# Second layer of a two-layer trunk: VectorE turns three of ten probability blocks of a head, and the low part of y moves to GpSimd

## The reference, cut to what matters

```python
for i in range(DEPTH):                       # 2 layers, 8 heads of 128, 512 tokens, width 1024
    hdn = rms_norm(x, norm_g[i])
    # layer 0: block attention with rotary; layer 1: forgetting attention
    q, k, v, z = split(hdn @ w_in)           # 1024 x 4096, per head 4 x 128 columns
    # layer 1, per head:
    sc = (q @ k.T) * scale + (c[..., :, None] - c[..., None, :])   # c: cumulative log-forget
    p = softmax(where(kpos <= tq, sc, -inf)) # 512 x 512, lower triangle
    y = p @ v
    x = x + (merge_heads(y) * silu(z)) @ w_out[i]
```

## Time and profile before

| | |
|---|---|
| median of 3 runs | 547.85 us (547.6 to 548.28) |
| the profiled execution | 548.04 us, span in the trace 546.0 us |
| PE busy | 538.5 us, 99% of the span |
| DVE busy | 411.2 us, 75% |
| ACT busy | 293.3 us, 54% |
| POOL busy | 301.6 us, 55% |

### The profile page before, as it was taken

The page is one execution under the profiler, slowest core; times in us unless marked ns, Lnnn a source line. Parts: engine busy times, 40 slices in busy tenths (PEclk is TensorE's granted clock), DMA queues, the critical chain, the costliest instruction groups (busy, mean ns, idle before and its releaser), DMA issues.

```text
span 546.0 us, 9781 instructions
## 1 busy us (share of the span) xinstructions
PE 538.5 (99%) x2963; PEld 498.4 (91%) x2963; DVE 411.2 (75%) x1042; ACT 293.3 (54%) x863; POOL 301.6 (55%) x357
## 2 busy tenths in 40 slices
PE   6999999999999999999999999999999999999998
PEld 5999999999999999888898999999999999998887
DVE  4678999999999999973563777878787878788331
ACT  6748282928282828272545473737374747464400
POOL 3874564646464646453645486747474747476300
PEclk9999999999999999999999999999999999999999
DMA  9914323231313131223513345525241534232021
GB/s 262 250 27 127 101 59 97 59 97 58 96 58 96 58 96 59 95 86 118 128 27 80 97 102 74 120 61 130 52 121 54 116 57 121 73 105 84 26 96 59
DMA packets 78540, 50.22 MB, mean 92 GB/s; under 512 B 4256, under 2 KB 71592, under 8 KB 78512
## 3 DMA queue, kind: packets, MB, share of 16 engines
q1 hardware_dynamic: 78496, 49.87, 33.8%
q10 hardware_dynamic: 16, 0.00, 0.0%
HBM read 47.75 MB, written 2.12 MB: 91 GB/s over the span
## 4 chain that ended last, share of the span: by engine, by line
PE 97%; DMA 1%; ACT 0%; DVE 0%; SPq 0%; issue 0%
PE banks L379 27%; PE banks L381 27%; PE banks L380 27%; PE banks L509 6%; PE banks L495 3%; PE banks L484 2%; PE banks L483 2%; PE banks L482 2%; DMA first_raw<-in_a_w_in_dram 1%; PE banks L416 1%; PE banks L536 0%; PE banks L535 0%; ACT hT_hi L670 0%; PE banks L467 0%; SPq L333 0%; DVE w_lo L885 0%
## 5 line engine op out<-in xcount | busy, mean ns | idle before, releaser
L1160 POOL TENSOR_TENSOR w_lo<-w_raw,w_hi 128x512 fp32r<-128x512 f32 x146 | 188.4, 1305 | 84.0 <-ACT w_hi L638 84.0
L379 PE MATMUL banks<-w_hi,hT_hi 128*128 128x384 f32 x512 | 173.5, 339 | 0.5 <-DVE w_lo L885 0.3
L381 PE MATMUL banks<-w_hi,hT_lo 128*128 128x384 f32 x512 | 171.8, 336 | 0.0
L380 PE MATMUL banks<-w_lo,hT_hi 128*128 128x384 f32 x512 | 171.8, 335 | 0.0
L947 DVE STREAM_TRANSPOSE banks<-qkn 32x256 f32<-32x256 f32 x240 | 109.4, 456 | 3.6
L379 PEld LDWEIGHTS banks<-w_hi,hT_hi 128*128 128x128 f32 x512 | 96.7, 189 | 2.3 <-DVE w_lo L885 0.7
L380 PEld LDWEIGHTS banks<-w_lo,hT_hi 128*128 128x128 f32 x512 | 96.7, 189 | 0.6
L381 PEld LDWEIGHTS banks<-w_hi,hT_lo 128*128 128x128 f32 x512 | 96.5, 189 | 0.0
L684 ACT ACTIVATE junk<-banks 128x128 bf16<-128x128 f32 x128 | 34.0, 272 | 112.0 <-PE banks L381 111.8
L638 ACT ACTIVATE w_hi<-w_raw 128x512 fp32r<-128x512 f32 x148 | 89.0, 638 | 8.9 <-PE banks L381 5.4
L1013 DVE RECIPROCAL gz<-gz 128x128 f32<-128x128 f32 x64 | 54.3, 908 | 0.7 <-ACT gz L736 0.7
(11 more groups left out here) (119 smaller groups left out, 915.9 us busy)
## 6 DMA issues: line engine op xcount, KB each, us to landing
w_raw<-in_b_w_in_dram SPq DMA_DIRECT2D x64, 256.0 KB, 3.6
w_raw<-in_a_w_in_dram SPq DMA_DIRECT2D x52, 256.0 KB, 2.9
w_raw<-in_w_out_dram SPq DMA_DIRECT2D x32, 256.0 KB, 2.7
first_raw<-in_a_w_in_dram SPq DMA_DIRECT2D x12, 256.0 KB, 5.7
cos_t<-c_rows SPq DMA_DIRECT2D x8, 256.0 KB, 3.6
out_dram<-xs SPq DMA_DIRECT2D x7, 256.0 KB, 2.0
xs<-in_x_dram SPq DMA_DIRECT2D x3, 512.0 KB, 5.9
xs<-in_x_dram SPq DMA_DIRECT2D x2, 256.0 KB, 3.1
```

Source lines behind the costliest of these rows:

```text
L379: pe.matmul(dst, ah, bh, start=first and m == 0, stop=False)
L380: pe.matmul(dst, ah, bl, start=False, stop=False)
L381: mm = pe.matmul(dst, al, bh, start=False, stop=last and m == n - 1)
L1160: pool.tensor_tensor(w_lo[:, slot, k, :], raw, f32(w_hi[:, slot, k, :]), ALU.subtract).then_inc(wlo_set, by)
```

## The change

Three edits, all in layer 1 and all for heads 0 to 6 (head 7 is left as it was, `by_dve` is false there).

1. PE's `turn_probs` leaves out the blocks of row tile 3 at key tiles 1, 2 and 3. DVE turns them in a new `turn_last_probs`, by 32x32 squares into the SBUF tile r_row: 16 transposes of 32x32 and 16 of 32x64. It stands behind `norm_qk` of tile 2 and ahead of `split_v` of tile 3, and signals last_turned.
2. ACT's and DVE's `split_probs` treat these blocks apart: in the second and third group the part from PE is read from PSUM, the part from DVE from r_row, so each engine has two instructions more. ACT waits for last_turned in the second group.
3. `low_y` in layer 1 moves from DVE, ahead of `silu_part`, to POOL, behind `rstd_qk` of tile 1.

```diff
+FIRST_BY_DVE = 1
+        def late_part(js):
+            return r_row[:, 0:P] if js[0] == 1 else r_row[:, P:3 * P]
+        def by_dve(layer, h):
+            return layer == 1 and not (isinstance(h, int) and h == HEADS - 1)
 # PE, turn_probs
                         for t in range(j, TILES):
+                            if by_dve(layer, h) and t == TILES - 1 and j >= FIRST_BY_DVE:
+                                continue
                             mm = pe.transpose(...)
 # ACT, split_probs
                     act.wait_ge(p_turned, 3 * g + n + 1)
-                    act.activation(pT_hi[:, c:c + w], banks[:, PT_AT[js[0]][0], 0:w], ACT.Copy).then_inc(pThi_set, 1)
+                    late = P * sum(j >= FIRST_BY_DVE for j in js) if by_dve(layer, h) else 0
+                    hi = act.activation(pT_hi[:, c:c + w - late], banks[:, PT_AT[js[0]][0], 0:w - late], ACT.Copy)
+                    if late:
+                        act.wait_ge(last_turned, h + 1)
+                        hi = act.activation(pT_hi[:, c + w - late:c + w], late_part(js), ACT.Copy)
+                    hi.then_inc(pThi_set, 1)
 # DVE, split_probs: likewise, a second subtraction that reads late_part(js)
 # DVE, new
+            def turn_last_probs(layer, h):
+                g = HEADS * layer + h
+                dve.wait_ge(probs_set, TILES * g + 1)
+                row = P_COL[TILES - 1]
+                for js in ((1,), (2, 3)):
+                    ...
+                    for a in range(QUADS):
+                        for b in range(QUADS):
+                            turned = dve.transpose(keys[b * QUAD:(b + 1) * QUAD, :, a * QUAD:(a + 1) * QUAD],
+                                                   tokens[a * QUAD:(a + 1) * QUAD, :, b * QUAD:(b + 1) * QUAD])
+                turned.then_inc(last_turned, 1)
 # DVE, period
-                if layer == 1:
-                    late_y(layer, h)
                 for n in range(4):
                     silu_part(layer, h, n)
                 split_v(layer, h + 1, 1 - s, 2)
                 norm_qk(layer, h + 1, 2)
+                if by_dve(layer, h):
+                    turn_last_probs(layer, h)
                 split_v(layer, h + 1, 1 - s, 3)
                 split_probs(layer, h)
 # POOL, period
-                if layer == 0 and not (isinstance(h, int) and h == 0):
+                if not (isinstance(h, int) and h == 0):
                     low_y(layer, h - 1)
```

More of the change, by code:

```diff
@@ L167, in build_trunk @@
         p_turned = sem("p_turned")
+        last_turned = sem("last_turned")
         pThi_set = sem("pThi_set")
@@ L987, in split_probs @@
                     dve.wait_ge(pThi_set, 3 * g + n + 1)
-                    dve.tensor_tensor(pT_lo[:, c:c + w], banks[:, PT_AT[js[0]][0], 0:w], f32(pT_hi[:, c:c + w]),
-                                      ALU.subtract).then_inc(pTlo_set, 1)
+                    late = P * sum(j >= FIRST_BY_DVE for j in js) if by_dve(layer, h) else 0
+                    lo = dve.tensor_tensor(pT_lo[:, c:c + w - late], banks[:, PT_AT[js[0]][0], 0:w - late],
+                                           f32(pT_hi[:, c:c + w - late]), ALU.subtract)
+                    if late:
+                        part = slice(c + w - late, c + w)
+                        lo = dve.tensor_tensor(pT_lo[:, part], late_part(js), f32(pT_hi[:, part]), ALU.subtract)
+                    lo.then_inc(pTlo_set, 1)
+            def turn_last_probs(layer, h):
[3 more added lines that the diff above has]
+                for js in ((1,), (2, 3)):
+                    if js[0] < FIRST_BY_DVE:
+                        continue
+                    n = len(js)
+                    tokens = probs[:, row + js[0] * P:row + (js[-1] + 1) * P].rearrange("p (j c) -> p j c", j=n)
+                    keys = late_part(js).rearrange("p (j c) -> p j c", j=n)
+                    for a in range(QUADS):
[3 more added lines that the diff above has]
+                turned.then_inc(last_turned, 1)
             def gate_y(layer, h):
```

## The result

The changed kernel takes 588.89 us (median of 5 runs, 587.69 to 590.47) against 547.99 us before: a ratio of 1.0746, 95% interval 1.0726 to 1.0766. It is slower by 41 us, and 14 us slower than the forecast of 575.

A forecast was written before the change was run, and what follows sets the result against it. TensorE, busy 99% of the span and 97% of the chain, was taken as the bound. First period 5.05, six periods of 3.65 and tail 0.5 make 27.4 us on 547.85: 575.3, range of all cases 561 to 580.

The forecast's parts named there:

- Part 1: PE's transposes: three fewer for each of seven heads save 2.3 us, the whole possible gain, 0.42%.
- Part 2, X: Time of DVE's 32 small transposes in a period, 222 and 256 ns each before small corrections, without overlap: 7.7 us.
- (a): Low weights behind ACT's wait are complete at E + 4.1, and PE's next qkv cannot start earlier.
- (b): Probabilities: two more DVE instructions add about 0.15; values can start at E + 2.0 and end at E + 3.95.
- E: End of DVE's last small transpose in a period: 25.6 if nothing else shifts, 26.6 with the loop closed.
- (c): Way round through DVE: norm of tile 0 makes the maxima start 1.0 later; period 30.7, 3.65 over 27.06.
- (d): Layer 1's first period, with no such delay behind it: period of 32.1, 5.05 over.
- (e): Passage into last: PE reaches the scores at about 7.5, DVE is ready at 8.0, costing 0.5.
- Part 3: Moving low_y from DVE to POOL: cost zero, by 0.1, covered by POOL's idle ahead of a weight chunk.
- Rivals 1 and 2: Small transposes overlap (3.65 us a period): 546.9, chance 0.06; each costs what a large one does (15.0): 626, chance 0.05.
- the estimate X = 4.0: Skill page's 1.0417 ns a column plus about 75 ns per instruction for DVE's transposes: 548 to 549 us.
- Rival 3: DVE's small transposes partly cheaper, between 4.7 and 6.9 us a period: 554 to 569 us, chance 0.12.

The follow-up runs named there:

- w67_first: Changed kernel with ACT's weight chunks 6 and 7 moved ahead of its split of the probabilities: 581.21 us, ratio 1.0596.
- warm_pe: Changed kernel with 16 matmuls of 512 columns that nobody reads filling PE's wait ahead of values: 579.79 us, ratio 1.0578.
- turn_only: Changed kernel without edit 3, so DVE turns three blocks and low_y stays on DVE: 588.31 us, ratio 1.0725.
- low_only: Kernel before with edit 3 alone: low_y on POOL in layer 1, PE turns all ten blocks: 548.85 us, ratio 1.0012.
- warm_w67: Changed kernel with 12 filler matmuls on PE ahead of values and ACT's weight chunks 6 and 7 ahead of its split: 573.78 us, ratio 1.0474.
- early_turn: Changed kernel with DVE's 32 transposes moved ahead of the gate's reciprocals, behind invert_sums: 601.85 us, ratio 1.0969.
- two_blocks: Changed kernel with DVE turning two of the ten blocks and PE eight: 552.31 us, ratio 1.008.
- unused_turns: Changed kernel where PE turns all ten blocks and DVE's 32 transposes are done but nobody reads them: 578.17 us, ratio 1.0533.
- two_w67: Changed kernel with DVE turning two blocks and ACT's weight chunks 6 and 7 ahead of its split of the probabilities: 558.64 us, ratio 1.0188.
- three_late_first: Changed kernel, three blocks on DVE, with DVE's subtractions from SBUF ahead of those from PSUM: 585.97 us, ratio 1.0697.

## Why the prediction was wrong

By its own steps:

- **Part 1**, PE's transposes: 139 of them are left, 2.3 us less work. Right, and without effect while PE waits.
- **Part 2, X**: 7.7 us forecast; the row at 423.20 has 7.44 for the 32. 202 and 236 ns against 211 and 245, 9 ns each, with 13 ns between them and no overlap. Right. The rule of the Trainium skill on held instructions, by which one whose input or output starts in another quadrant waits until the earlier ones have finished ("VectorE: DVE Perf Modes", section on two Vector instructions with no wait between them), agrees with these rows too.
- **(a) and (b), what follows E.** The mechanism held: ACT idled 5.12 in `split_probs`, the low weights are not what PE met last. A term was mis-sized: "two more instructions, about 0.15". From the first instruction behind E to `values` are 2.97 (430.68 to 433.65), not 2.0. The subtraction of 256 columns with both operands in SBUF took 1.38 beside POOL and 0.41 without it. These 0.97 are on every period; w67_first took back 7.7 us. The Trainium skill has the rule ("SBUF — State Buffer", section on the two separate sides): a DVE instruction with two SBUF inputs and a GpSimd instruction that reads SBUF hold a shared port exclusively, and the later one blocks for the whole of the other. The rows agree: 1.38 when it starts inside a POOL instruction, 0.41 when it starts behind one. The prediction had priced the two instructions by their columns.
- **The step that failed: (b), in two of its terms, and with it (c).** The first is the 0.15 just named, which measured 1.1. The second is that `values`, once started, "end at E + 3.95". Every sum took PE's work after a wait at the pace of before. After the waits of 3.4 us PE ran at PEclk 0.50, `values` took 3.7 to 3.9 in place of 1.92, and in every second head the first six matmuls of `qkv` were slow as well. In (c) the norm of tile 0 was to hold the maxima. It ended at 412.61, 12.0 after the start of `values`, as the forecast's loop has it (10.1 - 2.0 + 1.61 + 2.49 = 12.2), but PE's scores came later: the maxima started at 414.47, 13.87 after the start of `values`, and at 446.43, 12.78 after, in the head with the shorter slow stretch. The mean is 1.4 over 11.95. warm_pe, where the maxima start 11.95 after `values` (410.01 against 398.06), restored the forecast's loop: its periods are 31.16, and 30.7 - 0.3 for X + 0.97 for the subtraction is 31.4. It gave 9.1 us back.
- **(d)**: the first period's `values` came 0.5 later than forecast, which is 0.97 less 0.3 for X and 0.13 for a layer that began earlier (304.83 against 304.96). **(e)**: the tail from the last delayed `values` to the end is 57.7 where before it was 53.4 (492.58 to 546.0). Of the 4.3, 2.8 lie between these `values` and head 7's, which is what PE's slow stretch costs there; 0.65 of it was forecast. The other 1.5 are the last store: 3.7 from its issue at 584.52 to the end, where before it was 2.2 (543.80 to 546.0). In turn_only it is 2.2 again (584.28 to 586.5), so this belongs to the one profiled execution, which took 590.47 against a median of 588.89.
- **Part 3**: right; low_only and turn_only show it from both sides.

The sum with the measured terms: 0.5 for the first period, 6 x 1.8 = 10.8 for the periods (1.4 clock, 0.97 subtraction, -0.3 X, the rest unexplained at -0.3), 2.8 - 0.65 = 2.1 for the tail, 13.4 us. The median differs from the forecast by 588.9 - 575.3 = 13.6. The span of the profiled execution differs by 588.2 - 573.4 = 14.8, with the 1.5 of its last store. warm_w67, with both losses away, has 573.8.

Rivals 1 and 2 fall with the two rows of transposes. So does the estimate X = 4.0 that stands behind the rivals: 202 and 236 ns less 32 and 64 columns at 1.044 leave 169 ns an instruction, and nothing overlaps. Rival 3 had the small ones partly cheaper. They were, by 9 ns, too little for its case (X up to 6.9); whether the SBUF destination is the reason was not tried.

DVE's load says that three blocks could not be free, but not what they cost. In two periods of the changed kernel (columns as above):

```profile
400.60:433.65 33.05, 29.62 (x151) 27.83 (x151) 28.30 (x89) 15.46 (x50) 18.28 (x22) 0.91 0.27 71
433.65:465.61 31.96, 28.52 (x151) 26.79 (x151) 28.31 (x89) 15.46 (x50) 18.30 (x22) 0.93 0.32 74
```

DVE is busy 28.3 us a period, 7.3 more than before, and PE needs 26.73. Without the 0.97 of the long subtraction it is still 27.3, so no order of DVE's instructions brings three blocks under PE's pace. But periods are 32.5. DVE's load accounts for 28.3 - 27.05, 9 us over seven periods, of the 41; the rest comes from the order in which DVE, ACT, POOL and PE wait for each other, and from the clock. How near to 28.3 a better order of three blocks would come was not tried: early_turn and w67_first are two orders, both above 580. In two periods of two_blocks (400.00 to 454.68) it is busy 49.21, 24.6 a period. That fits under PE's 26.84 and the period is 27.34 all the same: the order decides, with 558.6, 552.3 and 549.6 us for three of them.

That a wait of 3.4 us brings the clock down, and one of 0.5 does not, is shown. Near 2 us the length alone does not decide: 2.04 in warm_pe kept the clock, 2.00 in unused_turns and two_w67 did not, and why was not tried. Nor was why the slow stretch is 5.6 us long in one head and 3.4 in the next.

## What to carry to other kernels

Before giving work to an engine that waits little, add up its busy time over the shortest repeating stretch and hold it against the bound engine's: here 21.0 + 7.4 passed 26.7, and a gain was out of reach. A sum that fits is not yet a promise, and one that does not fit gives only the least loss: what the engines wait for sets the period (two blocks, 24.6 us of load, 27.34 a period). When a forecast has the bound engine waiting, price what comes behind the wait too, by a row at the lower clock if one can be had; filler matmuls tell how much of a loss is clock. An instruction on VectorE with two SBUF operands is priced by what GpSimd does at that moment, and moving GpSimd's work is only a remedy if nothing else of GpSimd moves in.

## What the runs showed of the hardware

- Small transposes SBUF to SBUF: 202 ns for 32x32, 236 ns for 32x64, one every 215 and 249 ns.
- PE's granted clock went to 0.50 after idle of 2.00 (unused_turns, two_w67), 2.46 (w67_first), 2.66 (two_w67), 3.08 (three_late_first) and 3.4 us (the changed kernel), at once or within `values`. It stayed at 1.00 over idle of 0.2 and 1.74 (two_blocks), 0.5 and 2.04 (warm_pe) and 1.95 us (warm_w67).
- A subtraction on DVE with both operands in SBUF, 128x256: 0.41 to 0.43 us when it started with POOL idle. When it started inside a POOL instruction it took 0.47 to 1.44, by how much of that instruction was left, and each time ended about 0.3 us after it. POOL's next instruction was longer too (two weight chunks in 2.68, 2.54 without it).
